# A two-layer encoder step in split float32: one product order in every stage, and x's rows shifted by 0 to 128 bytes from stage to stage

## The reference, cut to what matters

```
def half_ffn(x, g, w_in, w_out):
    return x + FFN_RES * swiglu(rms_norm(x, g), w_in, w_out)
...
    yp = half_ffn(yp, ffn_norm1[i], ffn_w_in1[i], ffn_w_out1[i])
...
    yp = yp + op
...
    yp = half_ffn(yp, ffn_norm2[i], ffn_w_in2[i], ffn_w_out2[i])
```

## Time and profile before

| | us |
|---|---|
| median of 3 runs (1092.88 to 1095.26) | 1093.33 |
| the profiled execution's own time | 1096.32 |
| its span, first to last instruction | 1093.9 |
| TensorE busy in the span | 1077.1 (98%) |
| VectorE / ScalarE / GpSimd busy | 690.5 / 520.7 / 123.2 |
| DMA | 172.43 MB, 158 GB/s mean |

### The profile page before, as it was taken

The page is one execution under the profiler, slowest core; times in us unless marked ns, Lnnn a source line. Parts: engine busy times, 40 slices in busy tenths (PEclk is TensorE's granted clock), DMA queues, the critical chain, the costliest instruction groups (busy, mean ns, idle before and its releaser), DMA issues.

```text
span 1093.9 us, 21306 instructions
## 1 busy us (share of the span) xinstructions
PE 1077.1 (98%) x8086; PEld 1059.1 (97%) x8086; DVE 690.5 (63%) x1071; ACT 520.7 (48%) x812; POOL 123.2 (11%) x158
## 2 busy tenths in 40 slices
PE   8999999999999999999999999999999999999997
PEld 7999999999999999999999999999978899999997
DVE  7766665465655866665547666645599776666441
ACT  6544443355665644443335444433466554444332
POOL 4000001100004400000110000011232510000011
PEclk9999999999999999999999999999999999999999
DMA  6544454425333544454434444544332244444531
GB/s 231 197 179 161 156 209 159 140 105 183 131 126 126 192 186 155 180 192 159 165 146 155 165 180 153 203 158 154 136 120 90 100 170 159 180 159 182 184 133 43
DMA packets 24435, 172.43 MB, mean 158 GB/s; under 512 B 3236, under 2 KB 3400, under 8 KB 5832
## 3 DMA queue, kind: packets, MB, share of 16 engines
q1 hardware_dynamic: 22368, 167.45, 42.3%
q0 software_dynamic: 1248, 2.92, 0.7%
q10 hardware_dynamic: 776, 1.48, 0.4%
HBM read 169.28 MB, written 2.57 MB: 157 GB/s over the span
## 4 chain that ended last, share of the span: by engine, by line
PE 90%; DVE 5%; DMA 2%; ACT 2%; issue 1%; SPq 0%; POOL 0%; DVEq 0%; ACTq 0%
PE acc L409 85%; DVE wlo L391 2%; DMA raw<-in_w 2%; DMA x<-in_xT 1%; ACT whi L367 0%; DVE xs L1037 0%; PE mb L668 0%; PE mb L687 0%; DVE rstd L1042 0%; PE mb L594 0%; PE acc L715 0%; ACT work L955 0%; PE mb L429 0%; PE num L603 0%; DVE work L1264 0%
## 5 line engine op out<-in xcount | busy, mean ns | idle before, releaser
L409 PE MATMUL acc<-xs,whi 128*128 128x288 f32 x3392 | 601.1, 296 | 4.1 <-DVE wlo L391 2.2
L409 PEld LDWEIGHTS acc<-xs,whi 128*128 128x128 f32 x3392 | 510.3, 189 | 7.0 <-DVE wlo L391 2.4
L367 ACT ACTIVATE whi<-raw 128x1024 fp32r<-128x1024 f32 (+1 forms) x290 | 326.3, 1127 | 359.7 <-PE acc L409 332.6
L391 DVE TENSOR_TENSOR wlo<-raw,whi 128x1024 fp32r<-128x1024 f32 (+1 forms) x290 | 385.8, 1331 | 166.0 <-ACT whi L367 155.5
L409 PE MATMUL acc<-xs,wlo 128*128 128x288 f32 x1696 | 401.7, 295 | 0.6 <-DVE xs L1037 0.6
L409 PE MATMUL acc<-fs,whi 128*128 128x288 f32 x1664 | 290.3, 295 | 0.9 <-DVE fs L1276 0.7
L409 PEld LDWEIGHTS acc<-xs,wlo 128*128 128x128 f32 x1696 | 285.7, 189 | 0.9 <-DVE xs L1037 0.8
L409 PEld LDWEIGHTS acc<-fs,whi 128*128 128x128 f32 x1664 | 248.5, 188 | 1.9 <-DVE fs L1276 1.0
L409 PE MATMUL acc<-fs,wlo 128*128 128x288 f32 x832 | 192.6, 294 | 0.0
L409 PEld LDWEIGHTS acc<-fs,wlo 128*128 128x128 f32 x832 | 138.8, 188 | 0.0
L1064 DVE TENSOR_TENSOR work<-acc,rstd 128x288 f32<-128x288 f32 x88 | 40.2, 457 | 54.7 <-PE acc L409 54.2
(11 more groups left out here) (221 smaller groups left out, 470.1 us busy)
## 6 DMA issues: line engine op xcount, KB each, us to landing
raw<-in_w SPq DMA_DIRECT2D x113, 1024.0 KB, 4.7
raw<-in_w SPq DMA_DIRECT2D x32, 1408.0 KB, 5.8
x<-in_xT SPq DMA_DIRECT2D x4, 288.0 KB, 6.2
raw<-in_w SPq DMA_DIRECT2D x4, 256.0 KB, 5.8
work<-row_bounce ACTq DMA_DIRECT2D x1, 640.0 KB, 4.3
work<-in_cst POOLq DMA_DIRECT2D x1, 560.0 KB, 4.0
work<-in_c POOLq DMA_DIRECT2D x1, 514.0 KB, 5.9
out_cp<-work POOLq DMA_DIRECT2D x4, 128.5 KB, 4.0
```

What stands on the lines that cost most here:

```text
L367: act.activation(dst, src, ACT.Copy).then_inc(hi_done, 1)
L391: dve.tensor_tensor(dst, src, hi, ALU.subtract).then_inc(lo_done, 1)
L409: mm = pe.matmul(out, wt, xt, start=(first and n == 0), stop=(last and n == total - 1))
```

## The change

`PASSES` goes: `products()` makes hh, hl, lh of a tile and then the next tile, in all stages. And the rows of x no longer begin at the start of their padded row: `X_AT` gives a begin per normalisation, in floats, so that in stages 0, 2, 4, 6, 8 and 10 they begin 0, 16, 64, 128, 96 and 32 bytes further. The 288 floats still fit in the 320 of the row. The views `xhi`, `xlo` become `x_parts(norm)`, and every writer (L764, L818, L1037, L1095 of before) and reader (L409, L549) takes that view. The gate products of stage 2 read the rows shifted by 16 bytes.

```diff
-PASSES = {0: ("hh hl lh",), 1: ("hh hl lh",), 2: ("hh hl lh",), 4: ("lh hh hl",), 5: ("lh hh hl",), 6: ("hh hl", "lh"), 7: ("hh hl", "lh"), 8: ("hh hl lh",), 10: ("hh", "hl", "lh"), 11: ("hh", "hl", "lh")}
+NORM_OF = {0: 0, 2: 1, 4: 2, 6: 3, 8: 4, 10: 5}
+X_AT = (0, 4, 16, 32, 24, 8)
...
-        xhi, xlo = xs[:, 0, :, 0:T], xs[:, 1, :, 0:T]
...
+        def x_parts(norm):
+
+            o = X_AT[norm]
+            return xs[:, 0, :, o:o + T], xs[:, 1, :, o:o + T]
...
+        def products(pe, out, slot, tiles, hi, lo, first, last, before=None):
+
+            for n, (t, k) in enumerate(tiles):
+                if before:
+                    before(k)
+                wh, wl = whi[:, slot, t, :], wlo[:, slot, t, :]
+                pe.matmul(out, wh, hi[:, k, :], start=(first and n == 0), stop=False)
+                pe.matmul(out, wh, lo[:, k, :], start=False, stop=False)
+                mm = pe.matmul(out, wl, hi[:, k, :], start=False, stop=(last and n == len(tiles) - 1))
             return mm
...
-                products(pe, group_bank(g), c % 4, [(k, k) for k in range(KD)], xhi, xlo, True, True, None, PASSES[i]).then_inc(piece_done, 1)
+                products(pe, group_bank(g), c % 4, [(k, k) for k in range(KD)], *x_parts(NORM_OF[i]), True, True).then_inc(piece_done, 1)
```

More of the change, by code:

```diff
@@ L466, in first_two @@
                                 pe.wait_ge(evac, G + q - 3)
-                        mm = products(pe, group_bank(q), (c + q) % 4, [(k, k) for k in ks], xhi, xlo,
-                                      ks[0] == 0, ks[-1] == KD - 1, x_ready if q == 0 else None, PASSES[i])
+                        mm = products(pe, group_bank(q), (c + q) % 4, [(k, k) for k in ks], *x_parts(NORM_OF[i]),
+                                      ks[0] == 0, ks[-1] == KD - 1, before=x_ready if q == 0 else None)
                         if ks[-1] == KD - 1:
@@ L481, in very_first @@
                             pe.wait_ge(lo_done, q + 1)
-                        mm = products(pe, group_bank(q), q, [(k, k), (k + 1, k + 1)], xhi, xlo,
+                        mm = products(pe, group_bank(q), q, [(k, k), (k + 1, k + 1)], *x_parts(0),
                                       k == 0, k == KD - 2, before=x_ready if q == 0 else None)
@@ L512, in unit @@
                         products(pe, acc[u][:, 0:T], c % 4, [(t, t + 11 * q) for t in range(11)], ahi, alo,
-                                 q == 0, q == 1, before, PASSES[i]).then_inc(piece_done, 1)
+                                 q == 0, q == 1, before).then_inc(piece_done, 1)
                 unit(0, 0, before=lambda k: pe.wait_ge(alo_done, n_alo[0] + k + 1))
@@ L547, in gates @@
                 for k in range(KD):
-                    for n, xt in enumerate((xhi, xlo)):
+                    for n, xt in enumerate(x_parts(1)):
                         mm = pe.matmul(mb[0][:, 0:T], ghi[:, k, :], xt[:, k, :], start=(k == 0 and n == 0),
@@ L762, in hi_of_x @@
             def hi_of_x(m, norm):
-                act.activation(xhi[:, m, :], x[:, m, :], ACT.Copy, scale=norms[:, norm, m:m + 1]).then_inc(xhi_done, 1)
+                act.activation(x_parts(norm)[0][:, m, :], x[:, m, :], ACT.Copy, scale=norms[:, norm, m:m + 1]).then_inc(xhi_done, 1)
             def rms(done):
@@ L817, in unit @@
                     m = bass.ds(2 * it + u, 1)
-                    act.activation(xhi[:, m, :] if norm < N_FINAL else xg[:, m, :], x[:, m, :], ACT.Copy,
+                    act.activation(x_parts(norm)[0][:, m, :] if norm < N_FINAL else xg[:, m, :], x[:, m, :], ACT.Copy,
                                    scale=norms[:, norm, m]).then_inc(xhi_done, 1)
@@ L1036, in lo_of_x @@
                 dve.wait_ge(xhi_done, n)
-                dve.scalar_tensor_tensor(xlo[:, m, :], x[:, m, :], norms[:, norm, m:m + 1], xhi[:, m, :].bitcast(F32),
+                dve.scalar_tensor_tensor(x_parts(norm)[1][:, m, :], x[:, m, :], norms[:, norm, m:m + 1], x_parts(norm)[0][:, m, :].bitcast(F32),
                                          ALU.mult, ALU.subtract).then_inc(xlo_done, 1)
@@ L1094, in unit @@
                         dve.wait_ge(xhi_done, 2 * it + KD * norm + u + 1)
-                        dve.scalar_tensor_tensor(xlo[:, m, :], x[:, m, :], norms[:, norm, m], xhi[:, m, :].bitcast(F32),
+                        dve.scalar_tensor_tensor(x_parts(norm)[1][:, m, :], x[:, m, :], norms[:, norm, m], x_parts(norm)[0][:, m, :].bitcast(F32),
                                                  ALU.mult, ALU.subtract).then_inc(xlo_done, 1)
```

## The result

The change makes the kernel slower: median 1098.09 us (8 runs, 1096.45 to 1099.7) against 1093.83 us of before (8 runs, 1092.33 to 1097.03). The ratio is 1.0035, with a 95% interval of 1.0025 to 1.0046: 3.8 us, between 2.7 and 5.0 (the two medians lie 4.3 us apart). The profiled execution has a span of 1096.7 us where before had 1093.9.

What follows compares the result with a forecast made beforehand. TensorE was taken to bound the kernel, by the distance between matmul starts in four long stretches. Steps in stages 6, 10, 4, 2 and 8 summed to +6.2 us: 1093.33 + 6.2 = 1099.5 us, range 1094.9 to 1102.9.

Steps and rivals of the forecast that it cites:

- every shifted stage paying a step: The main case: each stage with shifted x rows streams 1.67 ns a product slower; 1098 to 1101 us, chance 0.50.
- One order in all stages, 0: All stages get the order hh, hl, lh with as many products and weight loads: 0, at worst 1 us either way.
- Writing x at shifted places, 0: ScalarE and VectorE write shifted x with as many instructions: 0, or 0.25 us if a shifted write cost 10% more.
- Stage 6, 128 bytes, +1.76: 1056 products of stage 6 take 1.67 ns more each, as low rows of fs do against the weights: +1.76 us.
- stage 10, 32 bytes, +1.76: 1056 products of stage 10 take 1.67 ns more each, as the gate products past ghi do: +1.76 us.
- one step: The 1.67 ns a product between 131.67 (equal begins modulo 256) and 133.3 (32 or 128 bytes apart), read as weight-load interference.
- Stage 4, 64 bytes, +1.76: No row shows 64 bytes; lying between 32 and 128, it was taken to cost stage 4 one step: +1.76 us.
- Stage 2, 16 bytes, +0.64: 384 of stage 2's products on the chain pay 1.67 ns each: +0.64 us, or 0; 0.64 was taken.
- stage 8, 96 bytes, +0.32: 192 of stage 8's products on the chain pay 1.67 ns each: +0.32 us.
- the faster rival: Stages 4, 10, 2 and 8 gain a step, stage 6 pays one: -2.7 us, 1090.6 us, chance 0.12.
- groups under 3.16 anywhere: A sign that would show the forecast wrong: a group of 24 products taking less than 3.16 us in any stage.
- The rival in which only some shifts pay: Two of stages 4, 6 and 10 pay, small ones or not: +3.5 to +4.5, 1096.9 to 1097.8 us, chance 0.14.

Runs made afterwards that it cites:

- undo_two: The changed kernel with the shifts of stages 6 and 10 put back to 0: 1094.42 us against 1094.46 of before, ratio 0.9999.
- best_48: The changed kernel with x at 48 bytes in all stages and fs at 16 in stages 1, 5, 7, 11: 1086.77 us against 1095.02 of before, ratio 0.9926.

## Why the prediction was right, and where not

The direction and the range were right: +6.2 us were forecast, +3.8 (2.7 to 5.0) measured, 1098.09 us where 1099.5 stood. But the case that was given 0.50, every shifted stage paying a step, did not occur: three of the five shifted stages paid nothing, and that 1098.09 still falls into its 1098 to 1101 is luck. By its steps:

- **What bounds it**: right. Only the distance between matmuls moved the time, in stages where TensorE was busy throughout before and after.
- **One order in all stages, 0**: right; alone it gives 0.9999.
- **Writing x at shifted places, 0**: right. VectorE's two instructions that make the low rows take 734 and 834 ns in the mean, 752 and 843 before.
- **Stage 6, 128 bytes, +1.76** and **stage 10, 32 bytes, +1.76**: right to the size, 133.3 ns a product, and the two of them are the whole loss. The rows they came from, a low row of fs against a high one and the gates, were the right neighbours, and the cause they were read for, the distance to the weight tile, is what the two kernels with moved tiles show. The "one step" of 1.67 ns is not a unit of the chip, though: 131.1, 132.5 and 134.7 are no whole steps from 131.67.
- **Stage 4, 64 bytes, +1.76**: wrong, 0. This is the step that carries most of the miss. It was interpolated between 32 and 128 as if pace changed slowly with distance; of the distances between, 48 bytes gave 130.0 or 132.5, 64 gave 131.7, 80 gave 131.1 and 112 gave 134.7. The execution of undo_two gave 64 bytes 0.56 ns more a product.
- **Stage 2, 16 bytes, +0.64** and **stage 8, 96 bytes, +0.32**: wrong in the same way. Stages 2 and 3 took 0.57 us less in the profile, stages 8 and 9 the same as before. Of the 0.57 pace explains some 0.2: in stage 2 one row of 95 products and two of 22 stand 130.0 ns apart, all others 131.6 to 131.9. At 96 bytes the products of stage 8 keep about 131.7.
- **"Nothing says that equal begins are the best case"**, the faster rival: it was right about the chip and wrong about this change. 130.0 exists, at 16, 48 and 144 bytes, but the change put only a part of stage 2 there. These groups of 3.12 us are one of the prediction's own signs of being wrong, "groups under 3.16 anywhere", and it came. The sign of the sum was to be decided by stage 10, and was.
- The rival in which only some shifts pay, two of the three big stages, came true: its +3.5 is what stages 6 and 10 cost (1.79 and 1.75 in the profile), and nearer to the 3.8 than the forecast's 6.2. It had been given 0.14.

The Trainium skill's rule of two independent read ports (TensorE: Matmul & The Clock Gate, Step-by-step: what each phase is for), by which loading the next tile takes nothing from the running matmul, can't be the whole of it here: lowering the weight tiles by 32 bytes modulo 256, with the streamed rows left where they were modulo 256, took the pace from 131.67 to 133.3 ns. That the weight load and the stream meet somewhere is my reading of this. No run took the weight load away or slowed it, so the mechanism stays open; that the distance decides which paces occur is shown.

What also stays open is which of its rhythms a stage falls into. It differs between stages of one execution that have the same distance and the same order, so these two don't settle it; what in the break of the stream does, no run shows.

## What to carry to other kernels

When matmuls stand back to back, read their distance from counts in long windows (0.16 ns in 110 us here) or, finer, from two starts and the number of products between them, and compare operands that differ in address only; one per cent can hang on where a streamed row begins relative to the weight tile. A price between two offsets can't be interpolated: measure each, and look at several executions, since one offset may have two paces. Here x at 144 bytes and fs at 16 from the weight tiles' begin, modulo 256, gave 0.9% for a few changed indices and 256 spare bytes a partition in each of two tiles.

## What the runs showed of the hardware that I had not expected

The pace of 288-column fp32r matmuls, each with its own weight load, takes separate values between 130.0 and 135.6 ns, depending on the distance of the streamed row from the weight tile, taken modulo 256. Long x stages of all profiles, mean distance of the starts in the windows above, ns a product:

| bytes further than the tile | seen in long stages |
|---|---|
| 0 | 131.7 (always) |
| 8 | 133.3 |
| 16 | 131.7 three times, 130.0 once |
| 32 | 133.3 (six times) |
| 40 | 135.6 |
| 48 | 130.0 seven times, 132.5 six times |
| 64 | 131.7 twice, 132.2 once |
| 80 | 131.1 |
| 112 | 134.7 |
| 128 | 133.3 (three times) |
| 144 | 130.0 four times, 131.1 once |
| 176 | 131.4 |
| 208 | 133.3 |

And for some distances the pace is chosen anew where the stream of products is broken, and then held, for over a hundred microseconds in the long stages: 48 bytes ran at 130.0 or 132.5, before and behind one such break in best_48's stage 6. The kernel with 48 bytes everywhere also has more widely spread runs, 9 us in place of 4 (before).
